# Second LayerNorm and combination spread over three engines, and keys turned into rows during routing, in a two-layer transformer block

## The reference, cut to what matters

```python
q, k, v, u = split_projection(h, w_in[l])
a = attention(q, k, v, ...)                  # two softmax maps per head, 4 heads
p = pool_mixer(u, ...)
h = layer_norm(ALPHA * h + concat(a, p) @ w_out[l], ln1_g[l], ln1_b[l])
h = layer_norm(ALPHA * h + moe_ffn(h, ...), ln2_g[l], ln2_b[l])    # top 2 of 16 experts
k_rows.append(k)                             # the keys themselves are an output
```

## Time and profile before

| | us |
|---|---|
| three runs | 1121.42, 1127.66, 1130.19 |
| median | 1127.66 |
| the profiled execution's own time | 1128.67 |
| its span in the profile | 1126.8 |
| PE busy | 976.5 (87%) |
| DVE busy | 839.6 (75%) |
| ACT busy | 633.1 (56%) |
| POOL busy | 193.8 (17%) |

### The profile page before, as it was taken

One profiled execution on the slowest core, in us unless ns is written; L12 is line 12 of the kernel. 1 busy time (PEld: TensorE's weight loads), 2 busy tenths in 40 slices (PEclk: granted clock), 3 DMA queues, 4 the chain that ended last, 5 costly groups with the idle time before them and its releaser, 6 DMA issues. The chain is left out here.

```text
span 1126.8 us, 14212 instructions
## 1 busy us (share of the span) xinstructions
PE 976.5 (87%) x4666; PEld 772.8 (69%) x4666; DVE 839.6 (75%) x1229; ACT 633.1 (56%) x898; POOL 193.8 (17%) x240
## 2 busy tenths in 40 slices
PE   3999899859999999999159998976999999999930
PEld 3988745347888888887159986545788888888820
DVE  8855446758989898987596554466789898898835
ACT  4344321137888888887334432102788888888720
POOL 4122320110121111100141223101011111111001
PEclk9999899959999999999669998995999999999975
DMA  9435540239999999996550356214799999999432
GB/s 349 167 104 187 178 175 24 81 135 309 366 378 360 370 358 356 367 360 241 189 192 29 107 194 241 106 49 180 242 363 365 367 360 370 368 363 353 162 144 81
DMA packets 120089, 273.02 MB, mean 242 GB/s; under 512 B 9414, under 2 KB 14910, under 8 KB 120014
## 3 DMA queue, kind: packets, MB, share of 16 engines
q1 hardware_dynamic: 96976, 230.18, 56.7%
q10 hardware_dynamic: 12510, 24.48, 6.3%
q0 software_dynamic: 10544, 17.65, 4.3%
HBM read 267.56 MB, written 25.92 MB: 260 GB/s over the span
## 5 line engine op out<-in xcount | busy, mean ns | idle before, releaser
L1149 DVE TENSOR_TENSOR w_lo<-ring,w_hi 128x1024 fp32r<-128x1024 f32 x256 | 299.0, 1220 | 38.0 <-ACT w_hi L1511 35.5
L1511 ACT ACTIVATE w_hi<-ring 128x1024 fp32r<-128x1024 f32 x256 | 260.5, 1060 | 42.0 <-PE PS L818 27.0
L783 PE MATMUL PS<-w_hi,x_hi 128*128 128x512 f32 x512 | 165.7, 405 | 8.8 <-DVE x_lo L1139 6.9
L788 PE MATMUL PS<-w_lo,x_hi 128*128 128x512 f32 x512 | 163.3, 400 | 0.0
L1156 DVE TENSOR_TENSOR w_lo<-ring,w_hi 128x1024 fp32r<-128x1024 f32 x128 | 155.6, 1221 | 9.4 <-ACT w_hi L1524 7.4
L783 PE MATMUL PS<-w_hi,x_lo 128*128 128x512 f32 x512 | 162.0, 397 | 0.0
L1524 ACT ACTIVATE w_hi<-ring 128x1024 fp32r<-128x1024 f32 x128 | 134.9, 1059 | 28.5 <-PE PS L788 28.5
L783 PEld LDWEIGHTS PS<-w_hi,x_hi 128*128 128x128 f32 x512 | 95.4, 192 | 31.0 <-ACT w_hi L1511 5.1
L783 PEld LDWEIGHTS PS<-w_hi,x_lo 128*128 128x128 f32 x512 | 97.8, 191 | 23.3
L788 PEld LDWEIGHTS PS<-w_lo,x_hi 128*128 128x128 f32 x512 | 97.2, 190 | 23.2 <-DVE w_lo L1149 0.6
L1754 POOL DMA_INDIRECT M<-xs,idx x32 | 53.2, 1664 | 294.9 <-PE PS L765 277.5
(11 more groups left out here) (202 smaller groups left out, 1510.4 us busy)
## 6 DMA issues: line engine op xcount, KB each, us to landing
ring<-in_w_gate SPq DMA_DIRECT2D x32, 2048.0 KB, 14.5
ring<-in_w_down SPq DMA_DIRECT2D x32, 2048.0 KB, 14.9
ring<-in_w_up SPq DMA_DIRECT2D x32, 2048.0 KB, 15.4
ring<-in_w_in SPq DMA_DIRECT2D x8, 2048.0 KB, 15.3
ring<-in_w_out SPq DMA_DIRECT2D x4, 2048.0 KB, 7.8
M<-in_cache_k ACTq DMA_DIRECT2D x8, 512.0 KB, 3.7
M<-in_cache_v ACTq DMA_DIRECT2D x8, 512.0 KB, 4.7
M<-ys ACTq DMA_DIRECT2D x4, 1024.0 KB, 7.0
```

The source lines that it names most:

```text
L783: pe.matmul(PS[:, n, :], x[:, c:c + P], w_hi[j][:, k * 512:(k + 1) * 512], start=(j == 0 and k == 0 and x is x_hi[par]), stop=False)
L788: mm = pe.matmul(PS[:, n, :], x_hi[par][:, c:c + P], lo[:, k * 512:(k + 1) * 512], start=False, stop=(j == 3 and k == 1))
L1149: dve.tensor_tensor(lo, w, w_hi[j][:, :].bitcast(F32), ALU.subtract).then_inc(up_lo, 1)
L1511: act.activation(w_hi[j][:, :], quarter(3 * par + n, j)[0], ACT.Copy).then_inc(up_hi, 1)
```

## The change

There are four parts.

1. The keys are no longer turned in attention. `keys_turned` does it in `route`: heads 0 and 1 ahead of the last tile's `turn_z`, heads 2 and 3 ahead of its logits, through the two PSUM banks of the output projection that are free then. ScalarE copies heads 0 and 1 before its `turned_h` of the last tile and heads 2 and 3 behind it, into a `kout` that holds all four heads, and `k_stored` sends them with three DMAs per layer behind the last exponential. Before the first expert ScalarE waits for these DMAs.
2. After the expert stage, H has already been multiplied by ALPHA (`h_prepared`, POOL, behind the gather for expert 3). The first scaled result is added to it by VectorE for tile 0 and by POOL for the others (`y_summed`), and VectorE adds gate 2 times the second result. In layer 0 VectorE moves two of the eight turned blocks to `FT` and ScalarE six.
3. In layer 1 gain and shift are split for tiles 0 and 1: VectorE subtracts the mean and multiplies by the gain, ScalarE multiplies by 1/deviation, POOL adds the shift (`h_shifted`). VectorE does tile 2 alone. SP's queue stores the tiles and waits for the stores.
4. The DMAs of all result rows are started before those of the gain and shift vectors.

Besides, `squared` waits for the squares of the unit before it.

```diff
@@ transposed_tasks: the list of TensorE's small tasks of attention
-            out += [[("k", h, "act")], [("past", h, "dve"), ("u", h, "act")], [("v", h, "act")]][j % 3]
+            out += [[], [("past", h, "dve"), ("u", h, "act")], [("v", h, "act")]][j % 3]
@@ tiles in SBUF
-        kout = M[:, 3648:4160].rearrange("p (t e) -> p t e", t=4)
+        kout = M[:, 2048:4096].rearrange("p (t e) -> p t e", t=4)
@@ before the engines' blocks
+        DVE_TURNS = [4, 4, 2, 4]
...
@@ sync, at its end
+            for j in tiles_of(DEPTH - 1):
+                dst = o["y_prompt"][0, P * j:P * (j + 1), :] if j < 2 else o["y_sample"].rearrange("b t n -> (b t) n")
+                sp.wait_ge(*((h_done, ln_count(LN2[-1], j)) if j < 2 else (h_last, 1)))
+                sp.dma_start(dst, H[:, j, :]).then_inc(y_out, 16)
+            sp.wait_ge(y_out, 48)
@@ tensor
+            def keys_turned(l, heads):
+
+                pe.wait_ge(res_done, 4 * l + len(order(LN1[l])) - 1)
+                for h in heads:
+                    if h >= 2:
+                        pe.wait_ge(k_kept, HEADS * l + h - 1)
+                    bank = 6 * (len(order(LN1[l])) % 2) + h % 2
+                    for x in range(4):
+                        mm = pe.transpose(PS[0:TN[x], bank, x * P:(x + 1) * P], kT[:, h, TC[x]:TC[x] + TN[x]], ident)
+                    mm.then_inc(k_turned, 1)
+
             def route(l):
                 last = len(order(LN1[l])) - 1
                 rank(l, last - 1)
+                keys_turned(l, (0, 1))
                 turn_z(LN1[l], last)
                 for n in range(last):
                     pe.wait_ge(hot_done, 4 * l + n + 1)
                     index_part(l, n, 5)
+                keys_turned(l, (2, 3))
                 logits(l, last)
                 rank(l, last)
+                pe.wait_ge(k_kept, HEADS * (l + 1))
                 totals(l)
@@ vector, after the expert stage
-                    dve.wait_ge(y_scaled, 4 * l + j + 1)
-                    then(dve.scalar_tensor_tensor(y[:, 0, :], y[:, 1, :], gates[0:n, j, 1:2], y[:, 0, :], ALU.mult,
-                                                  ALU.add))
-                    c = did(dve.scalar_tensor_tensor(H[0:n, j, :], H[0:n, j, :], ALPHA, y[:, 0, :], ALU.mult, ALU.add))
+                    h = H[0:n, j, :]
+                    if j == 0:
+                        dve.wait_ge(h_scaled, l + 1)
+                        dve.wait_ge(y_scaled, 4 * l + 1)
+                        then(dve.tensor_tensor(h, h, y[:, 0, :], ALU.add))
+                    else:
+                        dve.wait_ge(y_added, 3 * l + j)
+                    c = did(dve.scalar_tensor_tensor(h, y[:, 1, :], gates[0:n, j, 1:2], h, ALU.mult, ALU.add))
                     after(c)
                     dve.sem_inc(comb, 1)
                     ln_front(q, j)
                     if l + 1 == DEPTH:
-                        ln_h_gain(q, j)
-                        ln_h_shift(q, j)
+                        if j >= 1:
+                            ln_h_gain(q, j - 1)
+                            dve.sem_inc(h_gained, 1)
...
-                if l + 1 < DEPTH:
+                if l + 1 == DEPTH:
+                    ln_h_gain(q, 2)
+                    dve.scalar_tensor_tensor(H[:, 2, :], H[:, 2, :], stats[:, 2, 15:16], gb[:, 1, :], ALU.mult, ALU.add
+                                             ).then_inc(h_last, 1)
+                else:
@@ scalar
-                for k in range(4, KT):
+                for k in range(DVE_TURNS[q], KT):
...
+            def k_rows(l, heads):
+                for h in heads:
+                    c = slice(h * P, (h + 1) * P)
+                    bank = 6 * (len(order(LN1[l])) % 2) + h % 2
+                    act.wait_ge(k_turned, HEADS * l + h + 1)
+                    act.activation(kout[:, 0:3, c], PS[:, bank, 0:384].rearrange("p (t e) -> p t e", t=3), ACT.Copy)
+                    act.activation(kout[0:NMETA, 3, c], PS[0:NMETA, bank, 384:512], ACT.Copy).then_inc(k_kept, 1)
...
+                last = len(order(LN1[l])) - 1
                 for n, j in enumerate(order(LN1[l])):
+                    if n == last:
+                        k_rows(l, (0, 1))
                     turned_h(LN1[l], n)
+                    if n == last:
+                        k_rows(l, (2, 3))
...
-                act.wait_ge(k_out, 48 * HEADS * (l + 1))
+                k_stored(l)
+                act.wait_ge(k_out, 48 * (l + 1))
                 moe_round(l, rb, 0)
...
-                    if j == 0:
-                        load_gb(LN2[l], t["ln2_g"][l], t["ln2_b"][l])
+                load_gb(LN2[l], t["ln2_g"][l], t["ln2_b"][l])
...
                 for j in tiles:
                     scale_y(l, j)
+                if l + 1 == DEPTH:
+                    for j in range(2):
+                        act.wait_ge(h_gained, j + 1)
+                        act.activation(H[:, j, :], H[:, j, :], ACT.Copy, scale=stats[:, j, 15:16]
+                                       ).then_inc(h_normed, 1)
@@ gpsimd
+            def h_prepared(l):
+
+                for j in tiles_of(l):
+                    h = H[0:TN[j], j, :]
+                    last = pool.tensor_scalar(h, h, ALPHA, 0.0, ALU.mult, ALU.add)
+                last.then_inc(h_scaled, 1)
+
+            def y_summed(l, j):
+
+                h = H[0:TN[j], j, :]
+                pool.wait_ge(h_scaled, l + 1)
+                pool.wait_ge(y_scaled, 4 * l + j + 1)
+                pool.tensor_tensor(h, h, yb[j][0:TN[j], 0, :], ALU.add).then_inc(y_added, 1)
+
+            def h_shifted(q, n):
+
+                h = H[:, n, :]
+                pool.wait_ge(h_normed, n + 1)
+                pool.tensor_tensor(h, h, gb[:, 1, :], ALU.add).then_inc(h_done, 1)
...
@@ moe_round, behind the gathers for experts 0 to 3
+                if first:
+                    h_prepared(l)
...
                 for j in tiles:
+                    if j + 1 < len(tiles):
+                        y_summed(l, j + 1)
                     ln_power(q, j)
-                    if l + 1 == DEPTH:
-                        dst = o["y_prompt"][0, P * j:P * (j + 1), :] if j < 2 else o["y_sample"].rearrange(
-                            "b t n -> (b t) n")
-                        pool.wait_ge(h_done, ln_count(q, j))
-                        pool.dma_start(dst, H[:, j, :]).then_inc(y_out, 16)
+                    if l + 1 == DEPTH and j >= 1:
+                        h_shifted(q, j - 1)
...
-            pool.wait_ge(y_out, 48)
```

More of the change, by code:

```diff
@@ L304, in program @@
         round_closed = sem("round_closed")
-        y_scaled = sem("y_scaled")
+        y_scaled, y_added, h_gained, h_normed, h_scaled, h_last = (
+            sem("y_scaled"), sem("y_added"), sem("h_gained"), sem("h_normed"), sem("h_scaled"), sem("h_last"))
         y_in = [sem(f"y_in{i}") for i in range(4)]
@@ L351, in program, with turned_at @@
         LN2 = [2, 4]
+        DVE_TURNS = [4, 4, 2, 4]
+        def turned_at(q, n, k):
+            if q == LN2[0]:
+                d = DVE_TURNS[q]
+                first = 2 + 3 * (n % 2)
+                return (first, k * P) if k < d else (first + 1 + (k - d) // 4, (k - d) % 4 * P)
+            return (2 if q in LN1 else 2 + 2 * (n % 2)) + k // 4, k % 4 * P
         @block.sync
@@ L457, in turn_z @@
                 z = z_of(q)[n % 2]
-                for half in range(2):
-                    bank = 2 + half if q in LN1 else 2 + 2 * (n % 2) + half
-                    if q in LN1 and n >= 1:
-                        pe.wait_ge(hx_dve, 4 * q + n)
-                        pe.wait_ge(hx_act, 4 * q + n)
-                    for k in range(4):
-                        mm = pe.transpose(PS[:, bank, k * P:k * P + TN[j]],
-                                          z[0:TN[j], (4 * half + k) * P:(4 * half + k + 1) * P],
+                if q in LN1 and n >= 1:
+                    pe.wait_ge(hx_dve, 4 * q + n)
+                    pe.wait_ge(hx_act, 4 * q + n)
+                for ks in (range(DVE_TURNS[q]), range(DVE_TURNS[q], KT)):
+                    for k in ks:
+                        bank, at = turned_at(q, n, k)
+                        mm = pe.transpose(PS[:, bank, at:at + TN[j]], z[0:TN[j], k * P:(k + 1) * P],
                                           ident[0:TN[j], 0:TN[j]])
@@ L925, in turned_h @@
                     dve.wait_ge(early_in, 16)
-                for k in range(4):
+                for k in range(DVE_TURNS[q]):
                     c = C_LN + 16 * q + k
-                    last = dve.tensor_scalar(FT[:, k, TC[j]:TC[j] + TN[j]], PS[:, bank, k * P:k * P + TN[j]],
+                    bank, at = turned_at(q, n, k)
+                    last = dve.tensor_scalar(FT[:, k, TC[j]:TC[j] + TN[j]], PS[:, bank, at:at + TN[j]],
                                              CT[:, c:c + 1], CT[:, c + KT:c + KT + 1], ALU.mult, ALU.add)
@@ L1349, in turned_h @@
                 j = order(q)[n]
-                bank = 3 if q in LN1 else 3 + 2 * (n % 2)
```

(11 more changed lines are left out.)

38 lines of the change are left out of this document (14 added, 24 removed).

## The result

The changed kernel takes **1114.26 us** (median of 4 runs, 1112.42 to 1115.1) where the kernel before took 1128.93 beside it (1121.42 to 1130.78): ratio 0.9876, interval 0.9846 to 0.9906. That is 14.7 us faster, against a forecast of no change and a range that ended at 1118.

What follows compares the result with a forecast made beforehand. TensorE was taken to bound attention and experts, VectorE the stretch between layers and the end. Terms -3.9 + 4.0 + 5.1 + 0.8 - 6.1 = -0.1 us on 1127.66 gave about 1128 us, range 1118 to 1138.

Steps and rivals of the forecast that it cites:

- Keys out of attention: Attention: moving key transposes out saves TensorE 3.9 us over both layers; ScalarE's dropped copies and DMA issues save nothing.
- Routing: Before the last logits, transposes of key heads 2 and 3 cost 2.0 us a layer at half clock: +4.0.
- Experts: Second expert: POOL's scaling of H holds up VectorE's subtractions; TensorE loses 2.9 and 2.2 us: +5.1.
- The slower rival: Second expert: each POOL scaling pass holds VectorE 2.36 us, the stage pays 15; kernel at 1142 us, chance 10%.
- Between the layers: Between the layers: sums leave VectorE, ScalarE gets more turns of FT, and TensorE starts later: +0.8 us.
- the first race: Between the layers: POOL's first sum goes ahead of VectorE's next, which waits 2.3 us; had VectorE won, -1.4.
- The end: After the last expert: new schedule, SP's stores and POOL's earlier stop together shorten the span by 6.1 us.
- two bounds: Last 6.6 us of the span: tied to whatever ends last (-3.2) or to POOL's queue (-6.1); -6.1 was taken.
- Case 5: VectorE wins the first race and the scaling falls where VectorE is ahead; 1123 us, chance 8%.
- Case 1: Experts, between layers, end: POOL really runs beside VectorE, no expert stall; 1117 us, chance 10%.
- Case 3: Routing: key transposes fill TensorE's pause and the clock holds at 1.00 through the last logits; 1123 us, chance 10%.
- Case 2: End of the span: the last 6.6 us stay as they are; 1131 us, chance 22%.

Runs made afterwards that it cites:

- e3: Kernel before, with the three DMA issues of a head's key rows moved to the end of ScalarE's step, keys still turned in attention; 1124.21 us.
- e7: Changed kernel with key heads 2 and 3 turned behind the last tile's logits and copied behind the last exponential; 1112.93 us.
- e1: Kernel before with only the keys' part of the change, plus the wait in `squared`; 1121.96 us.
- e6: Changed kernel with POOL's scaling of H done twice, by the root of ALPHA each time, at the same place; 1117.1 us.
- e5: Changed kernel with POOL's scaling of H moved up, between the gathers for experts 1 and 2; 1113.78 us.
- e11: Changed kernel with all first sums (H plus first scaled result) on VectorE instead of POOL's passes; 1120.49 us.
- e9: Changed kernel with gain and shift vectors asked for right behind the first tile's result rows, as before the change; 1119.65 us.
- e4: Kernel before with SP storing the result rows and waiting for them, nothing behind POOL's last power; 1119.8 us.
- e8: Changed kernel with tile 1's last step done by VectorE in one pass instead of ScalarE and POOL; 1111.44 us.
- e10: Changed kernel with three moves together: earlier POOL scaling, key heads 2 and 3 behind the last logits, tile 1 finished by VectorE; 1106.81 us.

## Why the prediction was wrong

**The step that failed** is the sentence on ScalarE in "Keys out of attention": "it has slack there, so nothing." ScalarE is busy 34 of 80 us there, and that share said nothing of the 1.4 us in which three DMA issues held up a copy on TensorE's path. e3 removes the issues from that place and changes nothing else: TensorE's 1.22 us waits go, and attention of layer 0 is 1.9 us shorter at the same clock. In both layers the place of the sends is worth 3.5 us, where the forecast had 0. With 5.1 us instead of 3.9 for the turning the keys' part took 8.6 us out of attention at like clock, 4.7 more than forecast; with the 1.5 that isn't separated it was 10.1, 6.2 more. The prediction's own rule, that every instruction of a moved step counts, its DMAs too, was applied to the place where they went and not to the place that they left.

**Four other terms were off, all the same way**, so that nothing made up for it. In spans the change brought -14.8 us where the forecast had -0.1. Of these 14.7 us attention is 6.2, routing 1.5, the experts 2.5, the stretch between the layers 3.2 and the end 1.3. The failed step alone, 3.5 us, would have left the forecast near no change.

- Routing: +2.5 instead of +4.0. The mechanism was right; e7 shows it by taking it out. The price was 1.2 to 1.5 us a layer instead of 2.0. In layer 0 the clock fell later than before, so that the last turning of z took 0.4 us less; in e1, where the clock fell ahead of that turning, the price was 1.8. In layer 1 the logits had waited 0.2 us for VectorE anyway. The three key stores are 800 KB a layer, not 832; nothing rests on it.
- Experts: +2.6 instead of +5.1. The lock works as told: passes and subtractions alternate, TensorE pauses. A pass is 1.04 us and not 1.24, so a set of four costs 2.3 in layer 0, and layer 1 paid 0.5 for its three; the rest of the +3.8 and -1.2 isn't separated from where the clock stood. e6 doubles the cost in layer 0 (2.4 us more). e5 takes TensorE's pauses away, but a fall of the clock took most of their place. The slower rival (a pass as dear as a two-input one) is out: VectorE lost 4.6 us to seven passes, 0.66 each.
- Between the layers: -2.4 instead of +0.8. The forecast let POOL win the first race and put a price on the other way, -1.4. VectorE won it by 0.24 us (554.24 against 554.48). That would be 2.2 of the 3.2 us by the forecast's own price; no run made POOL win, so it is argued and not shown. e11 shows that the sums on POOL are worth 2.9 us there, and e9 that the earlier rows are worth 1.7, where the forecast said "help little".
- The end: -7.4 instead of -6.1. The schedule was nearly right: 20.6 us against 21.2, POOL and VectorE taking turns. VectorE's part is 3.6 us sooner (3.0 forecast), and the step behind it, the one taken as a choice between two bounds, came out as chosen: e4 alone shortened the tail by 6.3. As its text said, POOL's own ending stayed the last event (1105.86 to 1112.0, 6.1 us, for which it took 6.6), and POOL's shift ended 1.1 us before VectorE's, where the forecast had both end together. That brought 4.7 us instead of 3.1. e8 takes POOL's ending away and the end follows SP. Against this the first rows were scaled 0.9 us later behind the last scatter. The order of the loads isn't the reason: e9, with the old order, has 1.1 more than before, and e6, with the new one, none.

**The rivals.** The true case was none of the five. Case 5 (VectorE wins the race, the scaling falls where VectorE is ahead) came true in its first half, and in its second at most in layer 1. Case 1 had the right size, 1117, for the wrong reason: POOL and VectorE were not parallel. Case 3 failed: the routing stood at 0.51, though in layer 0 the clock fell 2.0 us later than before. Its text has the clock fall right behind TensorE's pause; in the trace it falls at 222.2, 0.9 us before the pause ends. Case 2 failed by e4. That the chance of faster by over 1% was put at only 7% follows from a sum in which the attention term had no upper bound of its own: a bound for "ScalarE has slack" would have been the three issues of 1.4 us at each of eight heads, up to 11 us.

**The rule on ports.** The statistics ran 1.29 us beside a 2.35 us POOL sum, and VectorE's two-input passes waited. By the Trainium skill (SBUF — State Buffer, "Who interferes with whom") a VectorE instruction with at most one SBUF input, outside the 2-port modes, doesn't contend with GpSimd, and the trace agrees: without POOL beside them the statistics took 1.28 us.

What stays open: how much of the 14.7 us is the place of the half-clock stretches. One profile per kernel shows attention of layer 0 between 0.96 and 1.00 and of layer 1 between 0.94 and 0.98. With the same code in layer 1 each 0.01 goes with 1 to 1.5 us (0.98 and 167.1 in e6, 0.97 and 168.5 in e1, 0.94 and 172.7 in e9).

## What to carry to other kernels

Read the queue and not the busy share: for every instruction that leaves a place, a DMA issue above all, ask what stood behind it and who waited for that; the view of waits of the engine that sets the pace names it in one row. Give "it has slack" a number in the range, as any other unknown cost. Give the last engine's own ending a row in the sum: which engine works last, and on which queue the last store stands, was worth 6.3 us by itself (e4), as much as the sums moved to POOL (6.3, e11).

## What the runs showed of the hardware

- **POOL ends late.** From the end of POOL's last work to the end of the span lie 6.1 us in the changed kernel (1105.86 to 1112.0), in e4, in e9 and in e11, whether that work is a long pass or a power; no row of the profile shows what fills it. From the end of SP's last issue to the span's end lie 2.7 us where SP is last (e8, 1107.94 to 1110.6; e10, 1101.88 to 1104.6). In e8 and e10 POOL stops 3.8 us before the last issue is done and SP is last; in e4 it stops 3.0 before and POOL is. By the difference, 6.1 less 2.7, POOL would have to stop about 3.4 us before SP's last issue is done: an estimate that lies between these cases.
- **A one-input POOL pass** of 1024 columns takes 1.02 to 1.04 us alone, and 2.0 beside two-input VectorE passes of 1.22: the two engines alternate.
- **The order of the loads sets when the second tile's rows come.** They were used 2.6 us behind the first tile's where the rows of all tiles were asked for first, 5.6 where the two vectors stood between (before), and 5.2 in e9. When the first tile's rows come doesn't follow the order: 4.9 us after their issue before and in e6, 5.4 in the changed kernel and in e9.
